# First weight piece issued from ScalarE's queue, and ScalarE's table load ahead of the parameter transfers

## What is computed

```python
proj = einsum('bsd,dc->bsc', x, w_in)
c_b, c_c, c_h, r_x, r_g = split(proj, 5 blocks of 512)
y_conv = c_b * conv3(c_c * c_h)
u = conv4(r_x) + lru_conv_b
y_lru = rg_lru(u, gates from w_rgate, w_igate, lru_lambda) * gelu(r_g)
x1 = layer_norm(alpha * x + concat(y_conv, y_lru) @ w_out)
logits = x1 @ w_router + b_router          # top 4 of 32, softmax of the four
ffn = sum over chosen e: gate_e * (swiglu(x1 @ w_gu[e] + b_gu[e]) @ w_dn[e] + b_dn[e])
out = layer_norm(alpha * x1 + ffn)
```

## Time and profile before

| | us |
|---|---|
| median of 3 runs | 1021.49 |
| lowest, highest | 1020.88, 1023.22 |
| the profiled execution's own time | 1020.78 |
| its span in the trace | 1019.0 |
| TensorE's matmuls, busy in the span | 824.2 (81%) |
| SP's queue, share of the 16 DMA engines | 98.0% |
| data moved over the span | 414 GB/s |

### The profile page before, as it was taken

The page is one execution under the profiler, slowest core; times in us unless marked ns, Lnnn a source line. Parts: engine busy times, 40 slices in busy tenths (PEclk is TensorE's granted clock), DMA queues, the critical chain, the costliest instruction groups (busy, mean ns, idle before and its releaser), DMA issues.

```text
span 1019.0 us, 20186 instructions
## 1 busy us (share of the span) xinstructions
PE 824.2 (81%) x8447; PEld 355.9 (35%) x8448; DVE 246.4 (24%) x692; ACT 79.5 (8%) x184; POOL 7.2 (1%) x25
## 2 busy tenths in 40 slices
PE   9999879898659999985699976666865885965995
PEld 7884433333213334331133421221321332311432
DVE  2473711221112222221112211111111221210233
ACT  1040100000000000000000000000000000000010
POOL 1000000000000000000000000000000000000000
PEclk9999989999899999998799998888989799988989
DMA  9988699999999999999999999999999999999996
GB/s 327 408 355 346 266 425 425 428 428 428 428 429 428 429 428 429 428 429 429 428 429 429 428 428 429 428 429 428 428 430 428 429 429 428 429 428 428 428 428 291
DMA packets 38903, 421.69 MB, mean 414 GB/s; under 512 B 5907, under 2 KB 6347, under 8 KB 14309
## 3 DMA queue, kind: packets, MB, share of 16 engines
q1 hardware_dynamic: 36436, 420.89, 98.0%
q10 hardware_dynamic: 2400, 0.44, 0.2%
q0 software_dynamic: 48, 0.09, 0.0%
HBM read 420.27 MB, written 1.18 MB: 414 GB/s over the span
## 4 chain that ended last, share of the span: by engine, by line
DMA 56%; PE 36%; DVE 5%; issue 2%; SPq 0%; DVEq 0%; POOLq 0%; ACT 0%; POOL 0%
DMA dn_buf<-in_w_down_dram 56%; PE ps L1038 12%; PE ps L1005 12%; PE ps L838 5%; PE ps L886 3%; PE ps L999 2%; PE ps L857 1%; DVE act_t L730 1%; DVE lin L725 1%; DVE lin L728 1%; DVE glu L722 1%; DVE lin L723 1%; DMA gu_buf<-in_w_in_dram 1%; PE ps L918 0%; PE ps L873 0%
## 5 line engine op out<-in xcount | busy, mean ns | idle before, releaser
L1005 PE MATMUL ps<-gu_buf,rows_t 128*32 128x512 f32 x2880 | 363.8, 651 | 102.0 <-DMA gu_buf<-in_w_gate_up_dram 102.0
L1005 PEld LDWEIGHTS ps<-gu_buf,rows_t 128*32 128x32 f32 x2880 | 93.8, 115 | 362.6 <-issue 196.0
L1038 PE MATMUL ps<-dn_buf,act_t 128*32 128x256 f32 x2848 | 171.1, 385 | 52.1 <-DMA dn_buf<-in_w_down_dram 44.1
L722 DVE TENSOR_SCALAR glu<-ps 128x256 f32<-128x256 f32 x45 | 19.1, 425 | 605.2 <-PE ps L1005 605.2
L1038 PEld LDWEIGHTS ps<-dn_buf,act_t 128*32 128x32 f32 x2848 | 87.7, 110 | 123.4 <-DMA dn_buf<-in_w_down_dram 59.2
L999 PE MATMUL ps<-turned,bias_sel 128*32 128x512 f32 x360 | 50.2, 630 | 22.6 <-issue 22.6
L449 ACT ACTIVATE sig<-glu 128x256 f32<-128x256 f32 x45 | 18.8, 417 | 529.1 <-DVE glu L722 529.1
L838 PE MATMUL ps<-turned,gu_buf 128*128 128x256 f32 x256 | 55.7, 379 | 0.0
L979 PE MATMUL ps<-mix,back 32*128 32x256 f32 x720 | 52.2, 404 | 0.5 <-ACT mix L453 0.5
L955 PE MATMUL ps<-xs,onehot 128*32 128x256 f32 x736 | 50.5, 394 | 1.5 <-DVE onehot L709 1.5
L838 PEld LDWEIGHTS ps<-turned,gu_buf 128*128 128x128 f32 x256 | 48.6, 190 | 6.9 <-issue 0.4
(11 more groups left out here) (234 smaller groups left out, 301.6 us busy)
## 6 DMA issues: line engine op xcount, KB each, us to landing
gu_buf<-in_w_gate_up_dram SPq DMA_DIRECT2D x128, 2048.0 KB, 30.2
dn_buf<-in_w_down_dram SPq DMA_DIRECT2D x62, 2048.0 KB, 13.3
gu_buf<-in_w_in_dram SPq DMA_DIRECT2D x4, 2048.0 KB, 18.4
gu_buf<-in_w_out_dram SPq DMA_DIRECT2D x2, 2048.0 KB, 16.9
dn_buf<-in_w_down_dram SPq DMA_DIRECT2D x2, 1024.0 KB, 27.1
xs<-in_x_dram SPq DMA_DIRECT2D x2, 512.0 KB, 5.4
gu_buf<-in_w_in_dram SPq DMA_DIRECT2D x2, 512.0 KB, 6.5
gu_buf<-in_w_in_dram SPq DMA_DIRECT2D x1, 1024.0 KB, 9.6
```

The source lines that it names most:

```text
L722: V.tensor_scalar(glu[:], half(HB, 0), SWIGLU_LIMIT, None, ALU.min).then_inc(S["glu_ok"], 1)
L1005: ins = T.matmul(ps[SLOTS * j:SLOTS * (j + 1), HB, :], rows_t[:, k, :], gu_buf[:, b, k, :].rearrange("p (two n) -> p two n", two=2)[:, :, ...
L1038: ins = T.matmul(ps[SLOTS * j:SLOTS * (j + 1), YB, 0:QF], act_t[:, DK * m + q, :], weights[q][:, QF * j:QF * (j + 1)], start=(m == 0 and q ...
```

## The change

In SP's stream the issue of the first weight piece is skipped (`if n:`), so x's second half and everything behind follow x's first half directly. ACT's stream gets three new lines at its front: it issues that same weight piece on its own queue, with the same semaphore; it waits for `quiet_ok`; and it copies one column of the cleared tile into a column of `sig`, which is overwritten later. The first activation instruction of the stream is what the table load is put in front of, so the load moves there from L392. The parameter transfers follow.

```diff
             for n, (k0, k1, landed) in enumerate(((0, 2, rx_in[0]), (2, 4, rx_in[1]), (4, KT, rx_in[2]))):
                 if n < 2:
                     sp.dma_start(xs[...PIECE * n:PIECE * (n + 1)], ...).then_inc(S[f"x_in{n}"], 16)
-                sp.dma_start(w_piece[:, piece_slot[RX], k0:k1, :], ...).then_inc(landed, 16)
+                if n:
+                    sp.dma_start(w_piece[:, piece_slot[RX], k0:k1, :], ...).then_inc(landed, 16)
         @block.scalar
         def _(act):
+            act.dma_start(w_piece[:, piece_slot[RX], 0:2, :], w_in_src[:, 0:2, COLS[RX]:COLS[RX] + PIECE]).then_inc(rx_in[0], 16)
+            act.wait_ge(S["quiet_ok"], 1)
+            nc.scalar.copy(sig[:, 0:1], quiet[:, 0:1])
             act.wait_ge(S["params_zero"], 1)
```

More of the change, by code:

```diff
@@ L235, in _ @@
                     sp.dma_start(xs[:, :, PIECE * n:PIECE * (n + 1)], x_src[:, :, PIECE * n:PIECE * (n + 1)]).then_inc(S[f"x_in{n}"], 16)
-                sp.dma_start(w_piece[:, piece_slot[RX], k0:k1, :], w_in_src[:, k0:k1, COLS[RX]:COLS[RX] + PIECE]).then_inc(landed, 16)
+                if n:
+                    sp.dma_start(w_piece[:, piece_slot[RX], k0:k1, :], w_in_src[:, k0:k1, COLS[RX]:COLS[RX] + PIECE]).then_inc(landed, 16)
             for i in (RG, CC, CH):
```

## The result

| | before | after |
|---|---|---|
| median of 20 runs, us | 1022.3 | 1024.18 |
| lowest to highest | 1020.86 to 1024.42 | 1021.84 to 1026.84 |
| span of the profiled execution | 1019.0 | 1022.8 |
| its own time | 1020.78 | 1024.55 |

The ratio of after to before is 1.0017, with a 95% interval from 1.0009 to 1.0024. The medians differ by 1.9 us: the change costs time, outside the noise of this many runs, and by just less than the 0.2% that I had called "no change".

What follows compares the result with a forecast made beforehand. The prediction took the chain of waits up to PE's first product at 6.92 us, then DMA from about 125 us, as the bound. +0.88 us there and 0 for all else gave 1022.3 us, range 1020.4 to 1024.6.

Steps and rivals of the forecast that it cites:

- The range: Whole kernel: 1020.4 to 1024.6 us, from 1021.3 and 1022.8 with the scatter of the runs around them.
- the sign of the likeliest case: Whole kernel: slower, by 0.88 us, between +0.5 and +1.34 us; chance 0.58.
- same: Whole kernel: a difference inside about 0.2%, or 2.0 us, not told from no change; chance 0.84.
- The sum: Whole kernel: +0.88 us at PE's first product, 0 for all else, passed to the end; 1022.3 us.
- x's delay: Kernel start: 179 packets of x's first half take turns with the weight piece's, 1.06 us, landing at 6.33.
- rival A: Kernel start: x lands undelayed at 5.27 us, PE's first product begins at 6.74; −0.18 us, 1021.3; chance 0.27.
- The first product: PE, kernel start: begins at 7.80 us, 0.88 us later than 6.92, behind ACT's copy of x.
- rival B: PE, kernel start: its clock falls in the longer gap before x; +3.5 us, 1025.0; chance 0.06.
- The table load, the new wait, the parameters' delay: ACT's stream, kernel start: moving the load, waiting for `quiet_ok` and issuing nine parameter transfers later each cost 0.
- rival C: ACT, kernel start: a parameter issue stalls 5.35 us and holds the copy of x; +4.1 us, 1025.6; chance 0.04.
- One for one to the end: From the start onward: DMA has no idle time from about 125 us, so any start shift reaches the end whole.

Runs made afterwards that it cites:

- change_again: The changed kernel profiled and timed a second time, nothing altered; median 1023.82 us, ratio to before 1.0019.
- piece_only: The changed kernel without the early table load and its wait, so only the weight piece moves to ACT's queue; 1023.74 us, ratio to before 1.0014.
- before_keep5: The kernel before with 5 throw-away products on PE where there were 7, no transfer moved; 1023.18 us, ratio to before 1.0012.
- half_piece: The changed kernel with the first weight piece cut in two, 256 KB on ACT's queue and 256 KB on SP's behind x's first half; 1024.22 us, ratio 1.0011.
- piece_late: The changed kernel with the whole weight piece issued behind the first two parameter transfers on ACT's queue; 1026.96 us, ratio to before 1.0041.
- before_keep9: The kernel before with 9 throw-away products on PE where there were 7; 1021.17 us, ratio to before 0.9989.
- change_keep11: The changed kernel with 11 throw-away products on PE where there were 7; 1022.97 us, ratio to before 1.0001.
- load_only: The kernel before with only the table load moved ahead of the parameter transfers, weight piece still on SP's queue; 1022.91 us, ratio to before 1.0001.

## Why the prediction was right where it was, and where not

**The range, the sign of the likeliest case and "same"** held: 1024.18 lies inside 1020.4 to 1024.6, at its upper end, and the difference of 0.17% is inside 0.2%. That is in part luck. The sum said +0.88 us and the medians say +1.88. The range was built for x's delay and the scatter of runs; it left out the clock, at 1025.0, and the clock is what came. It costs less in the medians than I had priced it, because before pays a part of it too, which I did not know.

**x's delay.** The step was 179 packets in turn at 5.9 ns, 1.06 us, x at 6.33. Measured: 6.18, 6.43 and 6.32 in the changed kernel, 0.94 to 1.19 us later than the 5.24 of before. Its parts held as well: 77 packets of x before the other queue's first (74 measured by 3.0 us), nearly one for one afterwards (274 to 231 from 3 to 6 us). This bears on rival A, which is gone: in no profile of a kernel that issues the piece at the start did x land as before. How exact the agreement is, is luck: the five kernels with the whole piece have x at 6.18 to 6.63, and for the halved piece the same sum gave 6.0 where 6.47 and 6.12 were measured.

By the Trainium skill, DMA: Bandwidth & Descriptors, section "Issuing engines are not separate DMA queues", issuing from a second engine saves only the time of the issue, and the traces agree that no rate was gained: 0.96 MB from 3 to 6 us against 0.95.

**The first product** was forecast 0.88 us late, and was 1.15, 0.95 and 1.30 us late. Where it is more, the excess is the transposes: four of them at the lower clock take 0.47 us more (the copy started 1.13 us after PE in after, 0.66 in before). Where they ran at the higher clock (change_again) the sum was right within 0.1 us.

**The term that failed is rival B's chance.** I gave the clock 0.06 and it is the rule: low in the first products in all three profiles of the changed kernel and in piece_only. My reason was a gap of 3.08 us deep in the program that had done no harm. One row could not bear that. The same gap, 2.45 to 3.08 us long, is in the other profiles too, and in six of the 14 (after, change_again, piece_only, before_keep5, half_piece, piece_late) the block behind it was slow. In after:

```profile
190.57 3.19 PE L1042 MATMUL ps<-dn_buf,act_t 128*32 128x256 f32 x32 [2.97 <-DMA dn_buf<-in_w_down_dram]
```

In the other eight it took 1.93 us, as in the earlier trace rows, six of them behind a gap just as long (2.95 to 3.08 us; the slow six had 2.93 to 2.97). So whether such a gap costs the clock differs from one execution to the next. At the start PE comes out of 3.4 us of throw-away products with nothing ahead of them; after 1.85 to 2.16 us of idle time it was in five profiles still at the lower clock and in two fell back to it. Worse, I took the kernel before to be clear of it, because its one profile was. It isn't in all its runs: before_keep9 beats it by 1.4 us in the median. So the price of B is not 2.6 us against nothing; it is the difference between a kernel that loses the clock in some runs and one that loses it in most. The profiled spans differ by 3.8 us, the medians by 1.9. change_keep11 is 0.85 us below change_again, so by that comparison about 1 us of the 1.9 would be x's delay. The other way to split it, change_keep11 against before_keep9, gives x's delay 1.8 us in the medians and 1.2 in the profiles. Both compare medians of twelve runs across two chips. That both causes are there is shown; their shares are not.

**The table load, the new wait, the parameters' delay** at 0: load_only agrees (1.0001). Nine parameter issues ended at 5.26 us (4.84 + 0.42), where I had 5.0, and ACT's copy waited for PE and not for them: rival C did not come.

**One for one to the end.** This held for the start itself, and better than the spans suggest. SP's issue of L286 at 122.57 us is at 125.80 in after (L287): 3.23 us, exactly the shift of L838. SP's issue at 601.76 us in before is at 605.56 in after, 3.80 us later, and the end shifted by 3.8. In before_keep5 the shifts are 1.11 us at 122 us, 1.15 at 602 (602.91) and 2.3 at the end; in change_again 2.67 (125.24), 4.95 (606.71) and 5.1. So nothing of a late start is made up for, and on top of it each profile lost something more later on: 0 to 3.0 us, if the table's spans are compared with its next blocks. The slow block at 190.57 us is one such place. Whether a late start brings the later losses about or chance does was not settled; before_keep5 lost its 1.2 us behind 602 us, with the shift unchanged up to there. The profile of before is of one of its fastest executions (1020.78 us, against a median of 1022.3), so differences of spans against it read too large for the typical run.

**Small slips of the prediction**, none of which moves the sum. x landed at 5.24 us and not at 5.27, which came from a duration rounded to 4.5. ACT had issued 14 transfers before 14.47 us (nine, then five) and not 13. With 0.6 us of scatter below A and 1.7 above 1022.8 the range would be 1020.7 to 1024.5.

## What to carry to other kernels

Giving the first transfer's competitor a queue of its own did not give it bandwidth of its own here: what is needed first should be first on one queue, and what is needed second behind it. Before a change at the start of a kernel is costed, ask how long TensorE will stand idle between its warm-up and its first real work; here 0.9 us more of waiting cost 2 us more in slow products in the profile of after. And look at the spread of the runs, not at one profile: a kernel whose runs scatter by 3 us may have a clock problem that its only trace does not show. Two more throw-away products (7 to 9) gained 0.11%, and the change under study lost 0.17%.

## What the runs showed of the hardware that I had not expected

- Two transfers issued on the two queues within 0.02 us do not start together: one sends its first packet 0.5 to 1.2 us behind the other. With equal sizes (512 KB each) SP's was first in five profiles of five, with 512 KB against 256 KB ACT's was first in two of two.
- The 16 completion counts of one transfer spread over 0.7 us (after) to 1.3 us (half_piece), and the last one decides when the waiting engine starts. An earlier first part does not bring an earlier landing.
- A transfer issued on ACT's queue at 1.99 us, when SP had issued three (x's two halves and a weight piece), had sent nothing by 5 us and landed 7.70 us after its issue; the same transfer issued at 0.78 landed after 5.8.
- After 3.36 us of throw-away products and some 2 us of idle time PE was at 1.2 GHz for L861's 16 records in part or in whole, which then took 5.41 to 5.77 us and not 3.69 (4.43 to 5.92 over all seven such profiles); the moment at which the clock rose differed between executions of one kernel.
- Near 190 us, the same gap of some 3 us (2.93 to 3.08) was followed by PE's lower clock in six profiles and not in six others.
- The granted clock reads 1.00 in the first microseconds of a trace even where the products' durations show the lower level (between 9 and 11 us of after, where the same kernel's other execution reads 0.50 at the same durations).
